# Two transformer blocks on one core: low halves between token tiles, identity transposes in the passages, other places for modulation fetches and for the experts' shares

## The chip, the core and the metric

The kernel runs on one core of a Trainium2 chip. The metric is the device time of one launch in microseconds; several launches of one build are made, and the median is given. Engines are named as in the profile: PE (TensorE), DVE (VectorE), ACT (ScalarE), POOL (GpSimd), SP (SyncE, which here only issues transfers).

## What is computed

The input is 256 tokens of width 1024 and one condition vector `c`. Two blocks follow each other, each of two layers.

```python
mods = einsum('bd,lde->lbe', silu(c), ada_w) + ada_b          # 6 vectors of 1024 per layer
for layer in range(2):                                        # first block
    sh1, sc1, g1, sh2, sc2, g2 = split(mods[layer], 6)
    h = rms_norm(x) * (1 + sc1) + sh1
    y = conv_fox_mixer(h) if layer == 0 else nsa_mixer(h)
    x = x + g1 * y
    h = rms_norm(x) * (1 + sc2) + sh2
    x = x + g2 * peer_ffn(h)          # 8 heads, 16 of 16384 experts each
for i in range(2):                                            # second block
    x = x + 0.5 * swiglu(rms_norm(x))                         # 1024 -> 2816 -> 1024
    x = x + concat(ssd(h), dilated_attention(h)) @ w_out      # h = rms_norm(x)
    x = x + 0.5 * swiglu(rms_norm(x))
```

In `peer_ffn` two key tables give 16 best scores each per head, their 256 sums give 16 picks, a softmax over the picks gives their shares, and each pick adds `share * gelu(x . u[e]) * v[e]`. The kernel computes it densely: all 16384 rows of `u` and `v` pass through PE, in tiles, and the shares are laid out as a sparse gate matrix.

## The kernel before

**Stages.** The program is a hand-scheduled list of instructions for each engine, with waits on semaphores. It goes through ten stages: mix0 (convolution and Fox attention), peer0, mix1 (the NSA mixer), peer1, ffnA0, ssd0, ffnB0, ffnA1, ssd1, ffnB1. The 256 tokens are two token tiles of 128. Activations stay in the chip's memory, and weights are streamed once.

**The ring.** All weights come as tiles of 128 x 1024 f32 (512 KB), named by their matrix and number: foxst (mix0's projections), foxo (its output), pq, pu, pv (the peer's queries, up and down), nsac, nsag, nsaq, nsak, nsaw, nsav, nsao (mix1) and so on. `sync_program` (L528) issues them on SP in one fixed order into the ring RING of NR = 5 buffers: tile n waits until tile n - 5 is used. The order is written out by the stages' lists, so everything on SP stands in one queue.

**Halves.** A product is made from a high half and a low half of both operands. ACT rounds each tile into HI (L506, NHL = 4 buffers), and DVE or POOL makes LOW = RING - HI (`lo_upto`, L519). The activations have the halves HTH and HTL. PE runs three products per tile: HTH with HI, HTL with HI, HTH with LOW (L772, L775, L780 in `project_two` for the first two tiles of a stage, L792 for the others, L810 and L843 for output tiles, L1960 and L1983 in the peer). Each is 8 matmuls of 128 x 256 or 4 of 128 x 512.

**Modulation.** The twelve vectors of the modulation are background work. `modulation_plan` ties items to tiles of the stream. A piece p has a "first" (POOL clears ACC at L551 and fetches the bias at L555), eight "slots" (DVE adds silu(c)_k times one 512 KB tile of ada_w to ACC, L571) and a "last" (PE sums over partitions at L600 or L606, and DVE finishes at L583 or L586). Pieces 2, 3, 4 lie in mix0 and piece 8 in mix1; their tiles don't go through the ring but into own buffers, nine in mix0 and four in mix1, fetched by SP at L535. `own_behind` says behind which ring tile, and an own fetch waits until the slot that had its buffer is done. The waits on SP, DVE and PE are in program order on each engine.

**Passage.** Between two stages the four quarters q = 2t + hf of the output y (token tile t, half hf) lie in four banks of the accumulation memory. `residual_vector` (DVE) first makes the LOW tiles up to the second tile of the next stage, then adds y to X: L890 in the second block, or L896 and L899 with a gate. ACT sums the squares (`norm_squares`, L656 for tile 0, L660 twice for tile 1), POOL takes the inverse roots (`norm_pool`, L671 to L681), DVE and ACT scale the rows (`norm_rows_vector` L688 for tile 0, L690 for tile 1, with ACT L663 for its last columns), and PE turns them in 8 transposes per token tile (`norm_tensor`, L706). ACT and DVE evict HTH (L722, L724, L743, L745), then HTL (L754, or L732 and L759 where there is a shift). PE has nothing else to do between the end of y and L706.

**The picks.** In the peer, `peer_experts` (DVE) finds, for token tile 0 and then for token tile 1, 16 top-16 lists over the keys, 8 over the sums and the experts' numbers, beside PE's up tiles j = 0 to 43. Behind tile SECOND_T = 44, ACT makes exp for both token tiles (L2104), and for each token tile in turn `peer_shares` makes the shares (L2197 to L2201), PE turns them (L2017), and DVE copies rows, columns and parts out (L2206 to L2214). Then the gates begin (L2233 to L2238 on DVE, L1946 on PE). exp and gelu are in different tables of ACT, and a change of table is an instruction of its own (ACT_TABLE_LOAD).

## Time and profile before

| | us |
|---|---|
| median of 3 runs | 3353.19 |
| lowest and highest | 3352.21, 3355.07 |
| the profiled execution | 3352.22 |
| its span, first to last instruction | 3350.4 |
| mean granted clock of PE, of full | 0.979 |
| busy: PE | 3200.2 (96%) |
| busy: DVE | 2408.6 (72%) |
| busy: ACT | 1662.8 (50%) |
| busy: POOL | 505.2 (15%) |

The profile is of one execution. The time of a run is some 2 us longer than the span. Busy times are sums over the span; matmuls overlap one another there and their ends are modelled, so a busy PE is not PE at its peak. The granted clock is given as a share of 2.4 GHz; 0.50 is 1.2 GHz. Line numbers are those of the kernel before.

### The profile page before, as it was taken

The page shows a single profiled execution, that of the slowest core. Times are in us where ns is not written, and L with a number is a line of the kernel's source. Part 1 is how long each engine was busy: PE and PEld are TensorE (multiplying, and loading weights), DVE is VectorE, ACT ScalarE, POOL GpSimd, SP SyncE. Part 2 cuts the span into 40 slices and gives each one's busy share as a digit, 9 for nine tenths or more (in the row PEclk, how much of TensorE's full clock was granted, in tenths as well). Part 3 has the DMA queues.
Part 4 walks back from the last instruction along what each step waited for, and adds up shares of the span by engine and source line. Part 5 has one row for each costly group of instructions (what it writes and reads, how often), then busy time and mean ns, then how long its engine had stood idle before and what let it go on. Part 6 is the DMA issues. An engine that isn't in the chain of part 4 may idle for free.

```text
span 3350.4 us, 56953 instructions
## 1 busy us (share of the span) xinstructions
PE 3200.2 (96%) x22530; PEld 2859.7 (85%) x22530; DVE 2408.6 (72%) x4140; ACT 1662.8 (50%) x2675; POOL 505.2 (15%) x363
## 2 busy tenths in 40 slices
PE   6899999999997889999999999999999999999999
PEld 6689877888887669987789998989869999898798
DVE  7879999776766569999966556558775555687754
ACT  3454555444454465455544544446554444465543
POOL 0269100000000258600000000001240000022300
PEclk8999999999998899999999999999999999999999
DMA  9445345677766215445566665555345655544355
GB/s 333 156 134 184 124 158 171 189 260 240 254 203 217 87 59 168 155 136 170 170 195 218 190 186 169 184 178 169 115 131 168 185 173 185 173 150 139 120 184 168
DMA packets 160534, 582.24 MB, mean 174 GB/s; under 512 B 18448, under 2 KB 20240, under 8 KB 160144
## 3 DMA queue, kind: packets, MB, share of 16 engines
q1 hardware_dynamic: 156528, 569.69, 53.3%
q10 hardware_dynamic: 3168, 8.35, 0.7%
q8 instruction: 181, 2.97, 0.3%
q0 software_dynamic: 576, 0.57, 0.1%
q14 instruction: 81, 0.66, 0.1%
HBM read 576.96 MB, written 1.05 MB: 173 GB/s over the span
## 4 chain that ended last, share of the span: by engine, by line
PE 86%; DVE 8%; ACT 2%; DMA 2%; issue 2%; POOL 1%; ACTq 0%; DVEq 0%; SPq 0%; POOLq 0%
PE P L1960 22%; PE P L792 21%; PE P L1983 21%; PE P L843 11%; PE P L1946 2%; DVE LOW L519 1%; DVE ssd_a L2768 1%; PE P L772 1%; PE P L706 1%; DVE mix_a L571 1%; ACT HI L506 1%; PE P L868 1%; PE P L775 1%; PE P L810 1%; PE P L1039 1%
## 5 line engine op out<-in xcount | busy, mean ns | idle before, releaser
L519 DVE TENSOR_TENSOR LOW<-RING,HI 128x1024 fp32r<-128x1024 f32 x882 | 1074.2, 1229 | 390.9 <-ACT HI L506 390.1
L506 ACT ACTIVATE HI<-RING 128x1024 fp32r<-128x1024 f32 x988 | 1037.2, 1053 | 388.9 <-DMA RING<-in_pu 157.5
L792 PE MATMUL P<-HTH,HI 128*128 128x256 f32 x2240 | 325.3, 288 | 18.8 <-ACT HI L506 13.9
L792 PE MATMUL P<-HTH,LOW 128*128 128x256 f32 x2240 | 317.2, 284 | 6.3 <-DVE LOW L519 6.1
L792 PEld LDWEIGHTS P<-HTH,HI 128*128 128x128 f32 x2240 | 291.9, 193 | 28.9 <-issue 18.7
L792 PE MATMUL P<-HTL,HI 128*128 128x256 f32 x2240 | 316.3, 284 | 0.0
L1960 PE MATMUL P<-HTH,HI 128*128 128x256 f32 x2048 | 299.8, 286 | 0.9 <-ACT HI L506 0.8
L792 PEld LDWEIGHTS P<-HTH,LOW 128*128 128x128 f32 x2240 | 290.3, 193 | 8.8 <-DVE LOW L519 8.8
L1960 PE MATMUL P<-HTL,HI 128*128 128x256 f32 x2048 | 291.0, 285 | 0.0
L792 PEld LDWEIGHTS P<-HTL,HI 128*128 128x128 f32 x2240 | 290.9, 193 | 0.0
L519 POOL TENSOR_TENSOR LOW<-RING,HI 128x1024 fp32r<-128x1024 f32 x106 | 279.0, 2653 | 62.4 <-ACT HI L506 62.4
L1960 PE MATMUL P<-HTH,LOW 128*128 128x256 f32 x2048 | 288.1, 284 | 0.0
L1960 PEld LDWEIGHTS P<-HTH,HI 128*128 128x128 f32 x2048 | 274.4, 191 | 14.4 <-issue 5.2
L1960 PEld LDWEIGHTS P<-HTL,HI 128*128 128x128 f32 x2048 | 265.2, 191 | 0.0
L1960 PEld LDWEIGHTS P<-HTH,LOW 128*128 128x128 f32 x2048 | 264.5, 191 | 0.0
L2052 ACT ACTIVATE peer_a<-P 128x256 f32<-128x256 f32 x256 | 97.7, 382 | 325.9 <-PE P L1960 325.8
L671 POOL TENSOR_SCALAR STAT<-STAT 128x1 f32<-128x1 f32 x10 | 2.2, 221 | 1100.0 <-DVE X L890 577.1
L2247 DVE TENSOR_TENSOR peer_a<-peer_a 128x256 f32<-128x256 f32 x256 | 159.4, 623 | 6.0 <-ACT peer_a L2052 5.9
L1983 PE MATMUL P<-LOW,peer_wh 128*128 128x512 f32 x512 | 150.2, 415 | 0.0
L551 POOL MEMSET ACC<- 128x1024 f32 x10 | 9.5, 954 | 923.7 <-PE P L1946 578.7
L2042 ACT ACTIVATE peer_a<-P 128x512 f32<-128x512 f32 x128 | 76.5, 597 | 134.2 <-PE P L1946 134.2
L1983 PE MATMUL P<-HI,peer_wh 128*128 128x512 f32 x512 | 138.2, 392 | 1.6 <-ACT peer_wh L2061 1.6
(434 smaller groups left out, 5101.5 us busy)
## 6 DMA issues: line engine op xcount, KB each, us to landing
RING<-in_pu SPq DMA_DIRECT2D x256, 512.0 KB, 3.9
RING<-in_pv SPq DMA_DIRECT2D x256, 512.0 KB, 3.6
RING<-in_ada SPq DMA_DIRECT2D x64, 512.0 KB, 4.8
...
```

The costliest lines, as they stand in the source:

```text
L506: act.activation(c.his[i % NHL], c.raw[m % NR], ACT.Copy).then_inc(*c.hi.at(("hi", m)))
L519: eng.tensor_tensor(c.low[m % NR], c.raw[m % NR], c.his[i % NHL].bitcast(F32), ALU.subtract).then_inc(*sig.at(("lo", m)))
L571: dve.scalar_tensor_tensor(out=acc, in0=c.own_tile(n) if own else c.raw[n % NR], scalar=c.silu_c[:, k:k + 1], in1=acc, op0=ALU.mult, op1=A ...
L706: m = pe.transpose(c.y[k // 2][:, k % 2 * 256 + t * 128:][:, 0:128], xn[:, t, k * 128:k * 128 + 128], c.const("ident"))
L792: m = pe.matmul(ps[:, 0:256], w[:, k * 128:k * 128 + 128], c.ht[h][:, k, :], start=i == 0 and k == 0, stop=i == 2 and k == 7)
L843: m = pe.matmul(c.y[q], lhs[1 if i == 1 else 0][:, t * 128:t * 128 + 128], (lo if i == 2 else hi)[:, hf * 512:hf * 512 + 512], start=i == ...
L1946: m = pe.matmul(f.gate_bank[:, 64 * t:64 * t + 64], f.is_row[g % 2][:, t // SIDE, :, t % SIDE], f.share[g % 2][q][:, t // SIDE, :, t % SID ...
L1960: m = pe.matmul(ps[:, 0:256], w[:, k * 128:k * 128 + 128], c.ht[h][:, k, :], start=i == 0 and k == 0, stop=i == 2 and k == 7)
L1983: m = pe.matmul(c.y[q], (f.wl(j) if i == 1 else f.wh(j))[:, t * 128:t * 128 + 128], (lo if i == 2 else hi)[:, hf * 512:hf * 512 + 512], st ...
L2042: act.activation(dst, c.psum(s, "gates", part, g).rearrange("p (t j) -> p t j", t=8), ACT.Copy, scale=1.0 / SHARE).then_inc(*c.act.at((s, ...
L2052: act.activation(f.act_of(c, j), c.psum(f.u, j)[:, 0:256], ACT.Gelu_apprx_tanh).then_inc(*c.act.at((f.s, "gelu", j), ("free", f.u, j)))
L2247: dve.tensor_tensor(ge, ge, f.gate_of(j), ALU.mult).then_inc(*c.dve.at((s, "weighed", j)))
```

## The change

It has four places.

1. In mix0 a modulation slot or another item is tied to every foxst tile but the first; before, foxst3 and foxst6 had none either. Later items come one or two tiles earlier, and the last sum (piece 4) two output tiles earlier. In mix1, piece 8 goes to nsac4 to nsac7 and nsaq0 to nsaq4 and nsaq6; before it had nsac2 to nsac7 and nsaq4 to nsaq7. `own_behind` places each own fetch at least five tiles behind the use that frees its buffer, and in mix1 the first ones behind nsac6.
2. `keep_clock` lets PE turn the identity matrix into a bank of its own: 28 times before it waits for the rows of token tile 0 in the passages into peer0, mix1, peer1 and ffnA0, 14 times in those into ssd0, ffnB0, ffnA1, ssd1 and ffnB1, and 3 times in all nine before the rows of token tile 1.
3. `residual_vector` makes the LOW tiles between token tile 0 and token tile 1.
4. In the peer, token tile 0's exp is made behind tile 28, its shares behind the 16 key lists of token tile 1, its transposes behind tile 34 and its parts behind the 8 lists of sums of token tile 1. Token tile 1 stays behind tile 44.

```diff
--- before.py
+++ after.py
@@ -16,7 +16,7 @@
 NR = 5
 NHL = 4
 AHEAD = {"act": 2, "dve": 1, "pool": 2}
-SECOND_T = 44
+EXP_T, FIRST_T, SECOND_T = 28, 34, 44
 SIDE = 2
 SHARE = 32768.0
 WHOLE = ("ada", "nsaw1")
@@ -336,14 +336,14 @@
             groups[10 * n + k].append(slots[k])
         groups[10 * n + 9].append(last)
     for t in FOX_ORDER:
-        if t[0] != "foxst" or t[1] > 8 or t[1] % 3:
+        if t != ("foxst", 0):
             after[t] = groups.pop(0) if groups else []
     assert not groups
     todo = of(6, 7, 9, 10, 5)
     spread(todo, [(("pv0", j), 1) for j in range(64, 127)])
     after["end", "peer0"] = todo
     todo = of(8)
-    spread(todo, [(("nsac", j), 1) for j in range(2, 8)] + [(("nsaq", j), 1) for j in (4, 5, 6, 7)])
+    spread(todo, [(("nsac", j), 1) for j in range(4, 8)] + [(("nsaq", j), 1) for j in (0, 1, 2, 3, 4, 6)])
     after["end", "mix1"] = todo
     todo = of(11)
     spread(todo, [(("pv1", j), 1) for j in range(64, 127, 3)])
@@ -411,12 +411,14 @@
             end = self.background.get(("end", s), [])
             self.stream += [(("ada", 8 * p + k), "") for what, p, k in end if what == "slot"]
         self.own_behind = {}
-        for order in (FOX_ORDER, [t for t, _ in stage_tiles("mix1")]):
+        for order, slots, begin in ((FOX_ORDER, OWN_SLOTS, 4), ([t for t, _ in stage_tiles("mix1")], OWN_LATE_SLOTS, 6)):
+            uses = []
             for place, t in enumerate(order):
                 for what, p, k in self.background.get(t, []):
                     if what == "slot":
-                        at = order[max(4, place - 3)]
-                        self.own_behind.setdefault(at, []).append(OWN.index(p) * 8 + k)
+                        free = uses[-slots] + 5 if len(uses) >= slots else begin
+                        self.own_behind.setdefault(order[max(free, place - 3)], []).append(OWN.index(p) * 8 + k)
+                        uses.append(place)
         self.place = {t: n for n, (t, _) in enumerate(self.stream)}
         assert len(self.place) == len(self.stream)
         halved = [n for n, (t, _) in enumerate(self.stream) if t[0] not in WHOLE]
@@ -691,14 +693,26 @@
         *c.dve.at((s, "rows", 1)))
 
 
+def keep_clock(pe, c, key, n):
+
+    ps = open_bank(pe, c, *key)
+    for k in range(n):
+        m = pe.transpose(ps[:, k % 4 * 128:k % 4 * 128 + 128], c.const("ident"), c.const("ident"))
+    m.then_inc(*c.pe.at(("free", *key)))
+
+
 def norm_tensor(pe, c, s):
 
     xn = norm_rows(c, s)
+    if s != STAGES[0]:
+        keep_clock(pe, c, ("clock", s, 0), 28 if s[:3] in ("pee", "mix") or s == "ffnA0" else 14)
     for q in range(4):
         if c.y_last[q] is not None:
             pe.wait_ge(*c.by("y_free", c.y_last[q], q))
         c.y_last[q] = s + "norm"
     for t in range(2):
+        if t and s != STAGES[0]:
+            keep_clock(pe, c, ("clock", s, 1), 3)
         pe.wait_ge(*c.by(s, "rows", t))
         for k in range(8):
             if t and k == ROWS_SPLIT // 128:
@@ -879,9 +893,9 @@
 def residual_vector(dve, c, s, name, scale, gate=None, gate_ready=None):
 
 
-    if s != STAGES[-1]:
-        lo_upto(dve, c, "dve", c.halved[c.turn[c.first_tile(STAGES[STAGES.index(s) + 1])] + 1])
     for t in range(2):
+        if t and s != STAGES[-1]:
+            lo_upto(dve, c, "dve", c.halved[c.turn[c.first_tile(STAGES[STAGES.index(s) + 1])] + 1])
         for hf in range(2):
             q = 2 * t + hf
             x = c.x[:, t, hf * 512:hf * 512 + 512]
@@ -2009,8 +2023,8 @@
             m.then_inc(*c.pe.at((s, "key_scores", t, hp)))
     for j in range(64):
         peer_up_tensor(pe, c, f, j, early_gates(j))
-        if j == SECOND_T:
-            for t in range(2):
+        for t in range(2):
+            if j == (FIRST_T, SECOND_T)[t]:
                 ps = open_bank(pe, c, s, "picks_turned", t)
                 pe.wait_ge(*c.by(s, "shares", t))
                 for q, src in enumerate((f.ei, f.ej, f.gg)):
@@ -2097,8 +2111,8 @@
         if j == 0:
             act.wait_ge(*c.by(s, "key_scores", 1, 3))
         peer_up_scalar(act, c, f, j)
-        if j == SECOND_T:
-            for t in range(2):
+        for t in range(2):
+            if j == (EXP_T, SECOND_T)[t]:
                 gg = f.gg[:, 128 * t:128 * t + 128]
                 act.wait_ge(*c.by(s, "shifted", t))
                 act.activation(gg, gg, ACT.Exp).then_inc(*c.act.at((s, "exp", t)))
@@ -2147,6 +2161,8 @@
         if h % 4 == 0:
             dve.wait_ge(*c.by(s, "scores", t, h // 4))
         top16(dve, c, sc[:, h, :], sv[:, h, :], si[:, h, :])
+    if t:
+        peer_shares(dve, c, f, 0)
     sf = f.sf[:, 256 * t:256 * t + 256]
     dve.wait_ge(*c.dve.last())
     dve.tensor_copy(sf.rearrange("p (q a h) -> p h q a", q=2, a=16), si.rearrange("p (h q) a -> p h q a", q=2))
@@ -2160,6 +2176,8 @@
     dve.wait_ge(*c.dve.last())
     for h in range(8):
         top16(dve, c, cd[:, h * 256:h * 256 + 256], cv[:, h, :], ci[:, h, :])
+    if t:
+        peer_parts(dve, c, f, 0)
     cit, cut = f.ci[:, 128 * t:128 * t + 128], f.cu[:, 128 * t:128 * t + 128]
     ca, cb = f.ca[:, 128 * t:128 * t + 128], f.cb[:, 128 * t:128 * t + 128]
     dve.wait_ge(*c.dve.last())
@@ -2200,6 +2218,10 @@
     dve.wait_ge(*c.dve.last())
     dve.tensor_tensor(gg, gg, st.unsqueeze(2).broadcast_to([128, 8, 16]), ALU.mult).then_inc(
         *c.dve.at((s, "shares", t)))
+
+
+def peer_parts(dve, c, f, t):
+    s = f.s
     dve.wait_ge(*c.by(s, "picks_turned", t))
     ps = c.psum(s, "picks_turned", t)
     for q, dst in enumerate((f.row, f.col)):
@@ -2262,8 +2284,8 @@
     peer_experts(dve, c, f, 0)
     peer_experts(dve, c, f, 1)
     feed(dve, c, "dve", f.u, SECOND_T)
-    peer_shares(dve, c, f, 0)
     peer_shares(dve, c, f, 1)
+    peer_parts(dve, c, f, 1)
     dve.wait_ge(*c.by(s, "parts", 1))
     for j in range(SECOND_T + 1, 64):
         for g in early_gates(j):
```

**SP, the start of mix1.** The order of the transfers before (nsac, nsag, nsaq are ring tiles, mix_a<-in_ada the own tiles of piece 8):

```order
L528 DMA RING<-in_nsac 128x1024 x5
L535 DMA mix_a<-in_ada 128x1024 x5
L528 DMA RING<-in_nsac 128x1024 x3
L528 DMA RING<-in_nsag 128x1024
L528 DMA RING<-in_nsaq 128x1024 x2
L535 DMA mix_a<-in_ada 128x1024
L528 DMA RING<-in_nsaq 128x1024
L535 DMA mix_a<-in_ada 128x1024
L528 DMA RING<-in_nsaq 128x1024
L535 DMA mix_a<-in_ada 128x1024
L528 DMA RING<-in_nsaq 128x1024 x4
```

and now:

```order
L530 DMA RING<-in_nsac 128x1024 x7
L537 DMA mix_a<-in_ada 128x1024 x4
L530 DMA RING<-in_nsac 128x1024
L530 DMA RING<-in_nsag 128x1024
L530 DMA RING<-in_nsaq 128x1024 x2
L537 DMA mix_a<-in_ada 128x1024
L530 DMA RING<-in_nsaq 128x1024
L537 DMA mix_a<-in_ada 128x1024
L530 DMA RING<-in_nsaq 128x1024
L537 DMA mix_a<-in_ada 128x1024
L530 DMA RING<-in_nsaq 128x1024 x2
L537 DMA mix_a<-in_ada 128x1024
```

Seven nsac tiles instead of five are issued ahead of the own tiles, four own tiles instead of five follow at once, and the later own tiles come one at a time between nsaq tiles.

**PE, the passage into ffnA1.** Before (L810 ends y, L706 turns the rows, L772 begins the next stage):

```order
L810 MATMUL P<-HI,ffnB_h 128x512
L810 MATMUL P<-HI,ffnB_l 128x512
L810 MATMUL P<-LOW,ffnB_h 128x512
L706 MATMUL P<-CST,ffnA_a 128x128 x16
L772 MATMUL P<-HTH,HI 128x256 x8
L775 MATMUL P<-HTH,LOW 128x256 x8
```

and now:

```order
L824 MATMUL P<-HI,ffnB_h 128x512
L824 MATMUL P<-HI,ffnB_l 128x512
L824 MATMUL P<-LOW,ffnB_h 128x512
L700 MATMUL P<-CST 128x128 x14
L720 MATMUL P<-CST,ffnA_a 128x128 x8
L700 MATMUL P<-CST 128x128 x3
L720 MATMUL P<-CST,ffnA_a 128x128 x8
L786 MATMUL P<-HTH,HI 128x256 x8
L789 MATMUL P<-HTH,LOW 128x256 x8
```

The 16 transposes have become 8 and 8, with 14 identity transposes ahead of the first 8 and 3 ahead of the second.

**DVE, the same passage.** Before (L519 makes LOW, L890 adds a quarter of y, L688 and L690 are the rows):

```order
L2370 TENSOR_TENSOR ffnB_l<-ffnB_a,ffnB_h 128x256
L519 TENSOR_TENSOR LOW<-RING,HI 128x1024 x23
L890 SCALAR_TENSOR_TENSOR X<-P,X 128x512 x4
L688 TENSOR_SCALAR ffnA_a<-X,STAT 128x1024
L690 TENSOR_SCALAR ffnA_a<-X,STAT 128x640
L743 TENSOR_SCALAR HTH<-P,CST 128x256 x4
```

and now:

```order
L2392 TENSOR_TENSOR ffnB_l<-ffnB_a,ffnB_h 128x256
L521 TENSOR_TENSOR LOW<-RING,HI 128x1024 x22
L904 SCALAR_TENSOR_TENSOR X<-P,X 128x512 x2
L521 TENSOR_TENSOR LOW<-RING,HI 128x1024
L904 SCALAR_TENSOR_TENSOR X<-P,X 128x512 x2
L690 TENSOR_SCALAR ffnA_a<-X,STAT 128x1024
L692 TENSOR_SCALAR ffnA_a<-X,STAT 128x640
L757 TENSOR_SCALAR HTH<-P,CST 128x256 x4
```

The last LOW stands between the two quarters of token tile 0 and those of token tile 1.

**DVE, picks of peer0.** Before, from the end of the experts (L2188) and LOW of the tile behind on:

```order
L2188 TENSOR_TENSOR peer_a<-peer_a 128x128
L519 TENSOR_TENSOR LOW<-RING,HI 128x1024
L2197 TENSOR_REDUCE STAT<-peer_a 128x8
L2199 RECIPROCAL STAT<-STAT 128x8
L2201 TENSOR_TENSOR peer_a<-peer_a,STAT 128x128
L2206 CAST peer_ij<-P 128x128 x2
L2209 TENSOR_SCALAR peer_g<-P 128x128
L2211 SCALAR_TENSOR_TENSOR peer_eq<-P,peer_g 128x128
L2214 CAST peer_g<-peer_eq 128x128
L2197 TENSOR_REDUCE STAT<-peer_a 128x8
L2199 RECIPROCAL STAT<-STAT 128x8
L2201 TENSOR_TENSOR peer_a<-peer_a,STAT 128x128
```

and now, first behind the key lists of token tile 1 (L2148, L2150 are parts of such a list, L2168 begins the sums):

```order
L2148 MAX peer_a<-peer_a 128x8
L2150 MAX_INDEX peer_a<-peer_a 128x8
L2215 TENSOR_REDUCE STAT<-peer_a 128x8
L2217 RECIPROCAL STAT<-STAT 128x8
L2219 TENSOR_TENSOR peer_a<-peer_a,STAT 128x128
L2168 CAST peer_a<-peer_a 128x8x32
L2171 TENSOR_TENSOR peer_a<-peer_a 128x2048
L2142 MAX peer_a<-peer_a 128x8
```

and from the end of the experts on:

```order
L2206 TENSOR_TENSOR peer_a<-peer_a 128x128
L521 TENSOR_TENSOR LOW<-RING,HI 128x1024
L2215 TENSOR_REDUCE STAT<-peer_a 128x8
L2217 RECIPROCAL STAT<-STAT 128x8
L2219 TENSOR_TENSOR peer_a<-peer_a,STAT 128x128
L2228 CAST peer_ij<-P 128x128 x2
L2231 TENSOR_SCALAR peer_g<-P 128x128
L2233 SCALAR_TENSOR_TENSOR peer_eq<-P,peer_g 128x128
L2236 CAST peer_g<-peer_eq 128x128
L2255 TENSOR_TENSOR peer_eq<-peer_iota,peer_ij 128x512
```

Behind the experts there is one leg of shares and parts instead of two, and the first gate (L2255) follows it.

## Rows read from the trace of the kernel before

**Rows 1.** The page's chain that ended last, by engine and line.

```profile
PE 86%; DVE 8%; ACT 2%; DMA 2%; issue 2%; POOL 1%; ACTq 0%; DVEq 0%; SPq 0%; POOLq 0%
PE P L1960 22%; PE P L792 21%; PE P L1983 21%; PE P L843 11%; PE P L1946 2%; DVE LOW L519 1%; DVE ssd_a L2768 1%; PE P L772 1%; PE P L706 1%; DVE mix_a L571 1%; ACT HI L506 1%; PE P L868 1%; PE P L775 1%; PE P L810 1%; PE P L1039 1%
```

**Rows 2.** The table of waits, PE: total, times, longest in us.

```profile
PE P L792 <- ACT HI L506: 13.9, 1, 13.9
```

**Rows 3.** Timeline of mix1's start: start, length, engine and line, [idle before <-releaser].

```profile
1023.99 18.29 SPq L535 DMA_DIRECT2D mix_a<-in_ada  x5
...
1036.31 1.19 POOL L1852 TENSOR_TENSOR mix_a<-mix_a 128x480 f32<-128x480 f32 x1 [19.95 <-DMA mix_a<-in_cmpb]
...
1040.65 1.28 DVE L571 SCALAR_TENSOR_TENSOR ACC<-mix_a,MOD,ACC 128x1024 f32<-128x1024 f32 x1 [8.51 <-issue]
1042.33 1.38 SPq L528 DMA_DIRECT2D RING<-in_nsac  x3
...
1047.99 2.05 PE L792 MATMUL P<-HTH,HI 128*128 128x256 f32 x8 [13.91 <-ACT HI L506]
...
1059.94 1.12 PE L792 MATMUL P<-HTL,HI 128*128 128x256 f32 x8
...
1060.90 1.12 PE L792 MATMUL P<-HTH,LOW 128*128 128x256 f32 x8
```

**Rows 4.** Windows of mix1: busy of PE, PEld, DVE, ACT, POOL; clock, DMA share, GB/s.

```profile
1022.00:1037.00 15.00, 12.08 (x101) 11.88 (x99) 9.64 (x20) 4.47 (x7) 0.69 (x1) 0.97 1.00 394
```

**Rows 5.** Windows of the passage into mix1, same columns.

```profile
1016.00:1019.00 3.00, 3.00 (x16) 2.97 (x15) 1.28 (x3) 1.70 (x4) 0.36 (x1) 0.50 0.00 0
```

**Rows 6.** Timeline, PE's transposes (L706) in the passages into mix1, ffnB0, ffnA1.

```profile
1015.52 3.56 PE L706 MATMUL P<-CST,mix_a 128*128 128x128 f32 x16 [4.65 <-DVE mix_a L688]
...
2511.48 3.65 PE L706 MATMUL P<-CST,ffnB_a 128*128 128x128 f32 x16 [2.86 <-DVE ffnB_a L688]
...
2707.02 1.07 PE L706 MATMUL P<-CST,ffnA_a 128*128 128x128 f32 x8 [2.76 <-DVE ffnA_a L688]
```

**Rows 7.** Timeline of the passage into ffnA1, DVE and ACT.

```profile
2701.36 1.22 DVE L519 TENSOR_TENSOR LOW<-RING,HI 128x1024 fp32r<-128x1024 f32 x1 [1.57 <-ACT HI L506]
...
2702.50 2.49 DVE L890 SCALAR_TENSOR_TENSOR X<-P,X 128x512 f32<-128x512 f32 x4
...
2703.81 1.06 ACT L656 ACTIVATE HTL<-X 128x1024 fp32r<-128x1024 f32 x1 [2.49 <-DVE X L890]
...
2707.70 0.55 DVE L690 TENSOR_SCALAR ffnA_a<-X,STAT 128x640 f32<-128x640 f32 x1 [0.82 <-POOL STAT L681]
```

**Rows 8.** Timeline of the passage into peer0.

```profile
177.40 1.84 PE L606 MATMUL P<-CST,ACC 128*128 128x1 f32 x16
179.28 0.17 DVE L586 SCALAR_TENSOR_TENSOR MOD<-P,CST 128x8 f32<-128x8 f32 x1 [5.49 <-PE P L606]
...
185.72 3.65 PE L706 MATMUL P<-CST,peer_a 128*128 128x128 f32 x16 [6.48 <-DVE peer_a L688]
```

**Rows 9.** Window of mix0's first products, columns as above.

```profile
53.00:80.00 27.00, 26.12 (x214) 25.51 (x213) 24.82 (x34) 9.86 (x15) 0.00 (x0) 1.00 0.93 336
```

**Rows 10.** Timeline of mix0, DVE.

```profile
128.34 1.28 DVE L571 SCALAR_TENSOR_TENSOR ACC<-mix_a,MOD,ACC 128x1024 f32<-128x1024 f32 x1 [2.68 <-issue]
```

**Rows 11.** Timeline behind tile 44 of peer0, PE and DVE.

```profile
353.26 0.73 PE L2017 MATMUL P<-CST,peer_a 128*128 128x128 f32 x3 [3.08 <-DVE peer_a L2201]
...
355.22 0.28 DVE L2197 TENSOR_REDUCE STAT<-peer_a 128x8 f32<-128x128 f32 x1
...
356.20 0.87 PE L2017 MATMUL P<-CST,peer_a 128*128 128x128 f32 x3 [2.21 <-DVE peer_a L2201]
...
358.42 0.43 DVE L2233 TENSOR_TENSOR peer_eq<-peer_iota,peer_ij 128x512 f16<-128x512 f16 x1
...
360.27 1.01 PE L1946 MATMUL P<-peer_pc,ACC 128*128 128x64 f16 x16 [2.34 <-DVE peer_pc L2238]
```

**Rows 12.** Timeline of peer0, ACT at tile 28.

```profile
304.15 0.38 ACT L2052 ACTIVATE peer_a<-P 128x256 f32<-128x256 f32 x1 [1.55 <-PE P L1960]
```

## The prediction

> **What bounds the kernel now.** I read the page's chain first: 86% of what ended last lies on TensorE (PE) [rows 1]. So an edit can pay in two ways only: it shortens a wait of PE, or a stretch in which PE runs on its lower clock. The table of waits says where to look: a single wait of 13.9 us for a high half [rows 2]. The timeline shows what stands behind it [rows 3], and the windows show the clock: 1.00 is 2.4 GHz, 0.50 is 1.2 GHz [rows 4, 5]. Everything below is summed against the profiled execution, 3352.22 us (span 3350.4); the median of the three runs is 1.0 us above it.
>
> **Part 1, the fetches in mix1: 12.5 us.** SP issues five nsac tiles and then five own ada tiles. The fifth has to wait until slot (8, 0) has freed its buffer, so that group stands on SP for 18.29 us, and nsac5 is fetched only at 1042.33. PE therefore starts nsac5 at 1047.99 after 13.91 us of waiting, and at the lower clock: 2.05 us for 8 matmuls, where a group at the higher clock takes 0.96 (from 1059.94 to 1060.90) [rows 3]. Slot (8, 0) itself was late, since it needs the bias, which POOL fetches only after L1852, and L1852 waited for in_cmpb until 1036.31 while the DMA engines were at a share of 1.00 [rows 3, 4].
> The change moves seven nsac tiles ahead of four own tiles and nothing on SP waits there. nsac5 and nsac6 are issued at about 1024 to 1025; behind them come four own tiles and nsac7. From 1024 on some 9 tiles of 512 KB and the rest of in_toep are moved at the 394 GB/s of that window [rows 4], 1.33 us a tile, so nsac7 lands by about 1040 and its three products could start at about 1041. DVE is the next limit. Slot (8, 0) stands in front of LOW of nsac7, and its bias comes about where it came (DVE L571 at 1040.65; I take up to 3 us later, because the memory set and bias moved behind nsac4 and nsac5 share the queues). So LOW of nsac7 is there by about 1045.1, and PE waits 1.6 to 3.3 us at nsac7, depending on how long the lower clock holds its first products back. Its LOW group and nsag's three follow, 4 x 0.96, at a clock not yet quite back: through at 1049.3. Before, nsag was through at 1061.9 [rows 3]. **Gain 12.5**, with ends 4 (the wait only moves, rival C) and 13.5 (slot (8, 0) comes on time). The moved slots stand in the q part, where DVE does 1.22 + 0.95 + 1.28 = 3.4 us a tile (LOW, the bias products, the slot) against about 3.6 of PE: cost 0, and were that cover gone, 0.2 for each of six tiles.
>
> **Part 2, the transposes: 10 us.** In each of the nine passages PE stops while DVE adds the residual and forms the first rows: 6.48 us (peer0), 4.65 (mix1), 2.86 (ffnB0), 2.76 (ffnA1) [rows 6, 8]; peer1 and ffnA0 are like mix1, the ssd passages like ffnB0. Behind that wait the granted clock is 0.50, for the 16 transposes and the first matmuls [rows 5]. At the lower clock 16 transposes take 3.65 us, 0.228 each; at the higher one 8 take 1.07, 0.134 each [rows 6]. 28 of the new ones are 3.8 us, 14 are 1.9, 3 are 0.4: at the higher clock all fit into the waits they stand in. So they cost nothing, if they count as work for the clock. That a row decides: in mix1 the clock came back at about 1019.0, just as the 16 transposes of L706, and nothing else, had run for 3.56 us [rows 5, 6]; in peer0 L706 runs 3.65 at 0.50 and is followed by the same return.
> What it gives: in ffnB0 the second rows are there at 2512.7 and their 8 transposes end at 2513.8 instead of 2515.1. Now the evictions bound it. HTH starts 0.9 to 1.0 earlier (ACT and DVE, 1.7 us each), the first four groups of matmuls end 2.0 earlier, HTL 1.0 earlier. Between 1.0 and 2.0 I take 1.5, for ffnA0, ffnB0 and ffnB1. ssd0 and ssd1 had the high clock for a part and get 1.15 each, ffnA1, whose first 8 transposes ran fast [rows 6], 1.05. In peer0, mix1 and peer1 the eight shifted columns on ACT (0.6 each) and their low parts follow one another; they start 0.7 earlier, and that is the gain: 3 x 0.7. **Sum 3 x 1.5 + 2 x 1.15 + 1.05 + 3 x 0.7 = 10**, ends 0 (rival B) and 14 (2.0 in the ffn kind).
> The Trainium skill ("TensorE: Matmul & The Clock Gate", section "Part 4: PE-mode transpose") speaks against this part: it says that the full clock does not engage for transposes, since they do not count as PE being busy in the same way. By that rule this term would be 0 and the sum 10 smaller; the rows of mix1 don't bear it out, but they can't exclude it, as matmuls followed at once.
>
> **Part 3, LOW between the token tiles: 3.2 us.** In ffnA1 DVE made LOW of the second next tile (1.22) up to 2702.5 and only then the four L890; ACT's squares of token tile 0 waited for the second of these until 2703.81 [rows 7]. y of tile 0 was complete over a microsecond earlier. Now tile 0 is added 1.2 earlier and LOW lies in front of tile 1, whose end stays at 2705.0. The squares start 1.2 earlier, the first rows 1.05 earlier. The two L660 of tile 1 then start on their data, 0.45 earlier than 2704.87 and 2705.48, and the second rows (2707.70) come about 0.6 earlier. Of that passage kind there are five: **5 x 0.6 = 3.0**; ends 0 and 5. In mix1 and ffnA0, where four pairs of 1.33 us bound DVE itself, it is 0.1 each. In peer0 and peer1 the LOW of the next stage is POOL's, nothing moves.
>
> **Part 4, modulation in mix0: 1.6 us.** The last sum (L606, 1.84 us on PE) stood at the end of mix0 and DVE waited for it with the whole residual, until 179.28 [rows 8]. It now runs two output tiles earlier. It stays on PE's path (y is 1.7 to 1.8 later there), but the residual starts with y: L606 takes over from the last matmul of L810 at 177.40 [rows 8], and y of the first quarter is there about 1 us before that. So it starts up to 2.7 earlier. DVE beside POOL's LOW is slower there, so I take **2.1**, ends 0 and 2.7. Against it: the two slots added behind foxst3 and foxst6 cost 1.28 each on DVE in a stretch where DVE is busy for 24.82 of 27 us and PE for 26.12 [rows 9]: at most 2.6, and half of it, 1.2, is taken; the waits for bias and slots at 124 to 138 (2.68 in front of L571 at 128.34 [rows 10]) come earlier and give 0.75 back. Net 1.6. The seven own tiles in one go behind foxst4, 9.3 us of traffic instead of 6.7, are ahead of a ring with five tiles in it: cost 0, or up to 2.6 if the ring runs dry.
>
> **Part 5, the picks: 3.4 us.** Behind tile 44 of peer0 PE waits 3.08 (L2017), 2.21 (L2017 again) and 2.34 (L1946) [rows 11]. Tile 1's leg runs from 355.22 to the first pick at 358.42, 3.2 us. With tile 0 done during tile 1's picks, only tile 1's leg is left behind tile 44, but DVE's experts end later: it waits about 1.1 for exp of tile 0, since ACT has gelu of tile 28 at 304.15 and then a table load and the exp, about 1.6, and it does the shares (355.22 until just before 356.20, 0.85) and the parts (1.3, up to 358.42) there [rows 11, 12]. So the experts end at about 352.3 instead of 349.0, LOW and tile 1's leg follow, and the picks start at 356.7: **gain 1.7** of the 3.2, ends 0 and 3.2. PE and DVE are both full for the 75 us behind, so a gain there carries. Two peers: 3.4. The two more table loads of each peer lie on ACT, which works for half of each tile: cost 0, and up to 2.6 a peer if ACT were the limit.
>
> **Sum**: 12.5 + 10 + 3.2 + 1.6 + 3.4 = 30.7 us, which gives 3352.2 - 30.7 = 3321.5, and with the 1.0 of the median **3322 us**.
>
> **Rivals.**
> A (my forecast, chance 0.67): as summed, within 3316 to 3328.
> B, the clock falls all the same (0.15): the transposes fit but the clock is 0.50 behind them. For it: the clock's return in mix1 may belong to the matmuls that followed at once. Against it: it came just as the transposes ended [rows 5, 6]. Part 2 then gives 0, and the overrun is small: 28 at 0.228 are 6.4 us against 4.65 of wait. Time: 3322 + 10 = 3332, and up to 3334 with the overrun.
> C, the wait in mix1 moves (0.12): slot (8, 0) is held up by the bias and LOW of nsac7 behind it, PE falls to the lower clock again, part 1 gives 4 instead of 12.5. For it: POOL's 19.95 us of waiting, which nothing in the change shortens [rows 3]. Against: two more tiles of work (5.8 us) are now ahead of it. Time 3322 + 8.5 = 3330.5.
> D, more than summed (0.04): ends above reached in parts 2 and 3: 3314.
> E, slower (0.02): SP's queue. It is one queue in fixed order, and the row of 18.29 us shows what an own fetch that waits for its buffer does to the ring behind it. In mix0, 15 of the 24 own fetches wait for a slot's release. If each of them held the ring for more than 30.7 / 15 = 2.0 us on PE's path, the gain is gone; at 2.5 us each the time is 3352 + 7 = 3359. Against it: with slots nine uses back and the fetch five places behind, the release is over long before; the page shows no such wait in mix0 now. That the change doesn't do what it says is excluded by the order of instructions, apart from B.
>
> **Numbers.** 3322 is the likeliest case's time. The range takes in B, C and a part of D: **3314 to 3334**; outside lie both B and C together (3340) and E. The measurement can tell 0.2%, 6.7 us, from no change. Faster by more than that: A to D, and B with C, 0.96; within 0.2% 0.02; slower 0.02.
>
> **What would show it.** Part 1: no wait of PE in front of nsac5, 1 to 4 us at nsac7, nsag through at about 1049 counted from mix1's start. Part 2: clock near 1.00 in the passages, L706 at 0.134 each, L700 at 0.134 too; were B right, L700 at 0.228 and clock 0.50. Part 3: the squares 1.2 and the second rows 0.6 earlier against the last y. Part 4: no wait of DVE for L606's sum in the passage. Part 5: one leg behind tile 44, picks 1.7 earlier against the end of tile 44. I am wrong if the time is above 3334 or below 3314, and wrong in the reasons if part 1 gives under 8 or part 2 under 5.

## The result, and the profile after

The changed kernel took 3335.3 us (median of 4, 3329.1 to 3336.9) beside 3353.5 (4 runs) for the kernel before: ratio 0.9949, 95% interval 0.9936 to 0.9962. On a second chip it was 3339.0 (5 runs) beside 3350.4 (10 runs), ratio 0.9965, 0.9951 to 0.9978. So 11 to 18 us were gained where the prediction had 31, and 3335.3 lies 1.3 us above the upper end of its range, 3339.0 lies 5.0 above it. The direction was right, the size was not.

The profiled execution took 3336.90 us (span 3335.1, mean granted clock 0.989 where it had been 0.979). Its page, the chain that ended last by engine and line (line numbers are now the changed kernel's, 2 to 22 higher):

```profile
PE 83%; DVE 10%; DMA 2%; ACT 2%; issue 2%; POOL 1%; ACTq 0%; DVEq 0%; POOLq 0%
PE P L806 22%; PE P L1997 20%; PE P L1974 19%; PE P L857 11%; PE P L1960 2%; DVE LOW L521 1%; DVE ssd_a L2790 1%; PE P L786 1%; DMA RING<-in_pv 1%; DMA RING<-in_pu 1%; PE P L824 1%; PE P L882 1%; ACT HI L508 1%; PE P L1053 1%; PE P L789 1%
```

PE's share fell from 86 to 83% [rows 1]; transfers for pu and pv have come in. In the table of waits the one wait of 13.9 us of [rows 2] has become three, 4.2 us together, the longest 2.9, and a line is there that was in no trace before, L1974 behind L2233:

```profile
PE P L2031 <- DVE peer_a L2219: 6.1, 2, 3.1
...
PE P L806 <- ACT HI L508: 4.2, 3, 2.9
...
PE P L1974 <- DVE peer_eq L2233: 3.6, 2, 1.8
```

**mix1.** The timeline (start, length, engine and line, [idle before <-releaser]):

```profile
1014.96 3.22 PE L700 MATMUL P<-CST 128*128 128x128 f32 x28
...
1029.53 1.93 SPq L537 DMA_DIRECT2D mix_a<-in_ada  x4
...
1033.28 0.33 SPq L530 DMA_DIRECT2D RING<-in_nsac  x1
...
1047.22 1.06 ACT L508 ACTIVATE HI<-RING 128x1024 fp32r<-128x1024 f32 x1 [6.06 <-DMA RING<-in_nsac]
...
1048.42 1.19 PE L806 MATMUL P<-HTH,HI 128*128 128x256 f32 x8 [2.88 <-ACT HI L508]
1048.57 1.28 DVE L573 SCALAR_TENSOR_TENSOR ACC<-mix_a,MOD,ACC 128x1024 f32<-128x1024 f32 x1 [4.87 <-issue]
```

These answer to [rows 3]. The own fetches are four and take 1.93 us on SP instead of 18.29. PE waits 0.56 us at nsac5 and 2.88 at nsac7, and not 13.91. ACT had to wait for the transfer of nsac7, which was issued at 1033.28 and landed at 1047.20. The identity transposes (L700) run at 0.115 us each (28 in 3.22), faster than the 0.134 I had taken.

**The passage into ffnA1**, against [rows 6, 7]: the turned rows take 1.07 and 1.09 and no transpose is at the lower clock.

```profile
2691.52 1.69 PE L700 MATMUL P<-CST 128*128 128x128 f32 x14
...
2693.35 1.07 PE L720 MATMUL P<-CST,ffnA_a 128*128 128x128 f32 x8
...
2695.01 1.09 PE L720 MATMUL P<-CST,ffnA_a 128*128 128x128 f32 x8 [0.27 <-DVE ffnA_a L692]
```

**The passage into peer0**, against [rows 8]. The residual starts at 178.8, as the prediction wanted, but two of its four L913 take 1.23 and 2.16 us instead of 0.69, while POOL makes two LOW tiles. The first rows stand at 187.09; before they stood at 185.72.

```profile
177.35 5.61 POOL L521 TENSOR_TENSOR LOW<-RING,HI 128x1024 fp32r<-128x1024 f32 x2 [5.50 <-ACT HI L508]
...
179.48 1.23 DVE L913 TENSOR_TENSOR X<-X,mix_a 128x512 f32<-128x512 f32 x1
...
181.35 2.16 DVE L913 TENSOR_TENSOR X<-X,mix_a 128x512 f32<-128x512 f32 x1
...
187.09 1.06 PE L720 MATMUL P<-CST,peer_a 128*128 128x128 f32 x8 [2.35 <-DVE peer_a L690]
```

**The picks of peer0**, against [rows 11, 12]:

```profile
307.12 0.29 DVE L2215 TENSOR_REDUCE STAT<-peer_a 128x8 f32<-128x128 f32 x1 [1.13 <-ACT peer_a L2118]
...
322.17 0.49 PE L2031 MATMUL P<-CST,peer_a 128*128 128x128 f32 x3
...
332.76 0.29 DVE L2233 SCALAR_TENSOR_TENSOR peer_eq<-P,peer_g 128x128 f32<-128x128 f32 x1
333.09 2.12 DVE L2236 CAST peer_g<-peer_eq 128x128 f16<-128x128 f32 x1
...
333.11 1.21 PE L1974 MATMUL P<-HTH,HI 128*128 128x256 f32 x8 [1.82 <-DVE peer_eq L2233]
...
356.59 0.61 PE L2031 MATMUL P<-CST,peer_a 128*128 128x128 f32 x3 [3.07 <-DVE peer_a L2219]
...
358.54 0.43 DVE L2255 TENSOR_TENSOR peer_eq<-peer_iota,peer_ij 128x512 f16<-128x512 f16 x1
```

Behind tile 44 one leg is gone, as forecast. But the first pick starts at 358.54 (before 358.42), in a trace that is 0.9 behind already at the start of the stage (rounding 36, below). DVE waits 1.13 for exp, as forecast; and PE, which turned tile 0's picks at 322.17, stands still for 1.82 us at 333.11 until DVE's L2233 has read them. The cast behind it takes 2.12 us, where tile 1's takes 0.23.

**Where the time went.** ACT rounds 988 tiles (L508, L506 before) in the same order in every kernel, so the starts of the same rounding can be set against one another in two traces. The table gives, for seven stretches between such starts, how much longer (+) or shorter than in the first profile of before they were, in us; the first row is counted from the start of the span. The last column is of kernels in which nothing of that stretch was touched (runs below).

| stretch (numbers of the roundings) | forecast | the change | again | untouched |
|---|---|---|---|---|
| mix0, passage into peer0 (0 to 36) | -2.3 | +0.9 | +2.4 | -0.2 to +2.3 |
| peer0 up to the down part, picks (36 to 180) | -1.7 | -1.1 | +1.0 | +0.1 to +0.6 |
| peer0, down part (180 to 292) | 0 | +4.4 | +2.2 | -1.3 to +5.1 |
| passage into mix1 and its start (292 to 317) | -13.3 | -10.2 | -8.9 | -0.3 to +0.6 |
| rest of mix1, passage into peer1 (317 to 336) | -0.7 | -1.6 | -0.5 | -3.4 to -0.9 |
| peer1 (336 to 588) | -1.7 | +0.1 | +1.3 | 0.0 to +0.8 |
| the second block (588 to 987) | -11.0 | -8.0 | -8.7 | -5.3 to 0.0 |

### The profile page after: what moved, and what is told of

Same layout as the page of the kernel before. It is cut to its first block, busy times and chain, and to the rows that moved or that the text cites. A ratio compares the mean times of both kernels' runs of the same rounds, so it can differ in the third digit from the quotient of the medians.

```text
span 3335.1 us, 57375 instructions
## 1 busy us (share of the span) xinstructions
PE 3218.4 (97%) x22739; PEld 2871.8 (86%) x22739; DVE 2410.0 (72%) x4140; ACT 1665.9 (50%) x2679; POOL 503.8 (15%) x363
## 4 chain that ended last, share of the span: by engine, by line
PE 83%; DVE 10%; DMA 2%; ACT 2%; issue 2%; POOL 1%; ACTq 0%; DVEq 0%; POOLq 0%
PE P L806 22%; PE P L1997 20%; PE P L1974 19%; PE P L857 11%; PE P L1960 2%; DVE LOW L521 1%; DVE ssd_a L2790 1%; PE P L786 1%; DMA RING<-in_pv 1%; DMA RING<-in_pu 1%; PE P L824 1%; PE P L882 1%; ACT HI L508 1%; PE P L1053 1%; PE P L789 1%
## 5 line engine op out<-in xcount | busy, mean ns | idle before, releaser
L508 ACT ACTIVATE HI<-RING 128x1024 fp32r<-128x1024 f32 x988 | 1035.6, 1053 | 374.7 <-DMA RING<-in_pu 153.3
L1974 PE MATMUL P<-HTH,HI 128*128 128x256 f32 x2048 | 300.4, 287 | 6.0 <-DVE peer_eq L2233 3.6
L806 PEld LDWEIGHTS P<-HTH,LOW 128*128 128x128 f32 x2240 | 291.1, 193 | 10.6 <-DVE LOW L521 10.6
L1974 PEld LDWEIGHTS P<-HTH,HI 128*128 128x128 f32 x2048 | 274.9, 191 | 20.0 <-issue 6.7
L1974 PE MATMUL P<-HTL,HI 128*128 128x256 f32 x2048 | 290.9, 285 | 0.0
L1974 PE MATMUL P<-HTH,LOW 128*128 128x256 f32 x2048 | 288.3, 284 | 0.0
L1974 PEld LDWEIGHTS P<-HTL,HI 128*128 128x128 f32 x2048 | 265.2, 191 | 0.0
L1974 PEld LDWEIGHTS P<-HTH,LOW 128*128 128x128 f32 x2048 | 264.5, 191 | 0.0
```

The lines of the kernel that those rows point to most:

```text
L508: act.activation(c.his[i % NHL], c.raw[m % NR], ACT.Copy).then_inc(*c.hi.at(("hi", m)))
L806: m = pe.matmul(ps[:, 0:256], w[:, k * 128:k * 128 + 128], c.ht[h][:, k, :], start=i == 0 and k == 0, stop=i == 2 and k == 7)
L1974: m = pe.matmul(ps[:, 0:256], w[:, k * 128:k * 128 + 128], c.ht[h][:, k, :], start=i == 0 and k == 0, stop=i == 2 and k == 7)
```

## The experiments

Each kernel was timed beside the kernel before on the same chip. The parts are those of the prediction. Single runs of every kernel, the one before too, scatter over up to 15 us, so differences of 2 to 3 us between medians tell little and smaller effects are read from one stretch of the traces.

**again**: the changed kernel once more.

> The changed kernel once more. Its profiled execution lost 4.3 us against before between the first down tile of peer0 and the passage into mix1, where the change alters no instruction; its four runs spread over 8 us. Theory 'traffic': that loss is chance of the transfers, so this profile shows another number there, the time lies anywhere in 3328 to 3337, and runs spread over several us again. Rival 'shift': the loss belongs to the kernel, it is 4 us there again (3 to 5).

3338.97 us (3335.8 to 3341.8), ratio 0.9965. The down part of peer0 was 2.2 longer than in the first profile of before, not 4.4. See before_again.

**before_again**: the kernel before once more.

> The kernel before once more, for a second profile. Between the first down tile of peer0 and the passage into mix1 (325 us, no instruction of it touched) eight profiles of other kernels took from 1.3 less to 5.1 more than the first profile of before. If that is chance of the transfers, this one lies in the same scatter, not at 0, and the time's scatter is as wide as the others' (8 us and more).

3351.34 us (3346.3 to 3357.9, 11 runs), ratio 0.9997 (0.9988 to 1.0006). The down part took 4.1 more than in the first profile with not one instruction changed. So the 4.4 us lost there by the change lie inside the scatter of a kernel that has no change in it; what varies there was not found. The two differences of medians, 18 and 11, hold such scatter too. The whole trace is 5.5 us longer at its last rounding.

**only_mix1**: the kernel before with part 1 alone.

```diff
-    spread(todo, [(("nsac", j), 1) for j in range(2, 8)] + [(("nsaq", j), 1) for j in (4, 5, 6, 7)])
+    spread(todo, [(("nsac", j), 1) for j in range(4, 8)] + [(("nsaq", j), 1) for j in (0, 1, 2, 3, 4, 6)])
```
(with the change's `own_behind` for mix1)

> The kernel before with only mix1's modulation plan and own fetches of the change. From the trace of the changed kernel: no fetch waits on SP, one wait of PE of 2 to 3 us at nsac7, gain of 10 to 12 us between the passage into mix1 and the one into peer1, nothing elsewhere. The part of peer0 behind the first down tile is as in the kernel before (0 within 1) if the 2 to 4 us lost there in all profiles of the change come from the change; if they are chance of the transfers it is 2 to 4 slower here too.

3339.59 us (11 runs), ratio 0.9972 (0.9963 to 0.9981), beside 3351.17: the medians differ by 11.6, the ratio says 9.4. In its trace the start of mix1 is 10.6 shorter, with waits of PE of 2.20 at nsac5 and 0.59 at nsac7, and the down part of peer0 0.7 longer, inside the scatter. Part 1 is most of what the change gives.

**own_later**: from pq_low_dve (below), the first own fetches of mix1 behind nsag.

```diff
-        ... [t for t, _ in stage_tiles("mix1")], OWN_LATE_SLOTS, 6)):
+        ... [t for t, _ in stage_tiles("mix1")], OWN_LATE_SLOTS, 8)):
```

> pq_low_dve with mix1's first four own fetches issued behind nsag instead of behind nsac6, so nsac7 and nsag are not behind 2 MB of them. Theory 'transfers' (nsac7 landed 15 us after its issue, and that is PE's last wait in mix1): nsac7's high half comes some 4 us earlier, PE's waits in front of nsac7 and its LOW go from 1.8 us to under 1, gain 0.5 to 2. Rival 'slot in front of LOW': slot (8, 0) stands ahead of LOW of nsac7 on DVE and its own tile now lands later, PE waits for that LOW instead, 0 to 4 us slower.

3334.76 us, ratio 0.9947 (0.9934 to 0.9960); the kernel it comes from had 0.9939, so no gain. The timeline shows both halves of the answer: ACT has nsac7 and nsag rounded by 1042.2, with no wait of PE left for the high half of nsac7, and then PE waits 3.90 us for LOW, since slot (8, 0), L573, comes first on DVE, at 1047.43.

```profile
1041.14 1.06 ACT L508 ACTIVATE HI<-RING 128x1024 fp32r<-128x1024 f32 x1 [0.21 <-DMA RING<-in_nsag]
...
1041.50 0.61 POOL L557 DMA_DIRECT2D ACC<-in_adab  x1 [0.29 <-POOL ACC L553]
...
1047.43 1.28 DVE L573 SCALAR_TENSOR_TENSOR ACC<-mix_a,MOD,ACC 128x1024 f32<-128x1024 f32 x1 [5.18 <-issue]
...
1049.90 1.94 PE L806 MATMUL P<-HTH,LOW 128*128 128x256 f32 x8 [3.90 <-DVE LOW L521]
```

The rival was right in the wait, not in what holds the slot: its own tile had landed at 1042.40, but its bias, fetched by POOL at 1041.50, landed only at 1047.35. In the changed kernel too the slot (1048.57) begins as its bias has landed (1048.49). So two things end at about the same time in front of nsac7, its transfer and the bias of the slot ahead of its LOW, and bringing the first forward alone gave nothing; the bias was not moved in any run. The stretch from 292 to 317 was 1.8 longer than in pq_low_dve.

**no_clock**: the change without the identity transposes.

```diff
-    if s != STAGES[0]:
-        keep_clock(pe, c, ("clock", s, 0), 28 if s[:3] in ("pee", "mix") or s == "ffnA0" else 14)
...
-        if t and s != STAGES[0]:
-            keep_clock(pe, c, ("clock", s, 1), 3)
```

> The changed kernel without the identity transposes. If they hold the clock: 0.50 stretches again behind the passages and 7 to 10 us slower than the changed kernel. If they do nothing for the clock (the rule that transposes don't count): same time within 2 us.

3339.36 us, ratio 0.9966 (0.9952 to 0.9979), beside 0.9965 with them: nothing by the medians. The trace says why. In ffnA0 the clock fell and 16 transposes took 3.65; in ffnA1, with LOW between the token tiles, PE waits only 1.67 and both groups run at the higher clock without any help (L716 is the turning of rows here):

```profile
2052.55 3.65 PE L716 MATMUL P<-CST,ffnA_a 128*128 128x128 f32 x16 [4.53 <-DVE ffnA_a L690]
...
2693.94 1.07 PE L716 MATMUL P<-CST,ffnA_a 128*128 128x128 f32 x8 [1.67 <-DVE ffnA_a L690]
2695.61 1.09 PE L716 MATMUL P<-CST,ffnA_a 128*128 128x128 f32 x8 [0.60 <-DVE ffnA_a L692]
```

The time is the one that was expected if the transposes did nothing, but the reason is another: the transposes do hold the clock (only_clock), and where the earlier LOW had already shortened the wait there was little left to lose. Of the five passages behind ffnA0 only ffnB0 still lost the clock, for its second rows (1.66).

**only_low**: the kernel before with LOW between the token tiles alone.

```diff
-    if s != STAGES[-1]:
-        lo_upto(dve, c, "dve", ...)
     for t in range(2):
+        if t and s != STAGES[-1]:
+            lo_upto(dve, c, "dve", ...)
```

> The kernel before with only LOW moved between the token tiles. Theory 'covered twice': PE's idle time before the first rows falls from 2.8 to 1.7 in the second block's five plain passages, the clock stays at 1.00 in most of them, and the five give 4 to 7 us together, more than the 3.0 of the prediction; mix1, ffnA0 and the peers give 0. Rival: rows come 0.6 earlier and the clock falls as before, 3.0.

3347.54 us (12 runs), ratio 0.9993 (0.9985 to 1.0002). The second block is 5.9 shorter than in the first profile of before. By the time, a gain isn't clear of noise. The wait in front of the first rows of ffnA1 is 1.66 instead of 2.76 [rows 6], and both groups of transposes run fast:

```profile
2703.85 1.07 PE L706 MATMUL P<-CST,ffnA_a 128*128 128x128 f32 x8 [1.66 <-DVE ffnA_a L688]
...
2705.52 1.09 PE L706 MATMUL P<-CST,ffnA_a 128*128 128x128 f32 x8 [0.60 <-DVE ffnA_a L690]
```

**only_clock**: the kernel before with the transposes alone.

> The kernel before with only the identity transposes. Theory 'covered twice': the transposes hold the clock in all nine passages, but without them the earlier LOW already keeps it in four of the five passages of the second block, so alone they give 1.0 to 1.5 us in each of ffnA0, ssd0, ffnB0, ffnA1, ffnB1 and about 0 in ssd1, 5 to 7 us in those six. Rival 'no gain': the evictions bound the passages and the six give under 2.

3348.12 us (12 runs), ratio 0.9987 (0.9978 to 0.9997). All transposes of rows from mix1 to ffnB1 take 1.06 to 1.09 a group; in peer0 the first group still took 1.94. In ffnA0, whose 16 row transposes took 3.65 in no_clock:

```profile
2062.55 3.22 PE L698 MATMUL P<-CST 128*128 128x128 f32 x28
...
2067.54 1.07 PE L718 MATMUL P<-CST,ffnA_a 128*128 128x128 f32 x8 [1.77 <-DVE ffnA_a L688]
...
2069.03 1.09 PE L718 MATMUL P<-CST,ffnA_a 128*128 128x128 f32 x8
```

The second block is 7.5 shorter. But in three kernels in which neither the transposes nor LOW were touched it was also shorter than in the first profile of before: 1.5 (only_mix0), 3.1 (only_mix1), 5.3 us (only_picks). A part of the reason stands in ffnB0, where only_mix1 has the instructions of before. It turned its first rows at the higher clock after the same wait of 2.84 us, where [rows 6] has 16 at the lower after 2.86 (L708 is L706 of before):

```profile
2499.45 1.06 PE L708 MATMUL P<-CST,ffnB_a 128*128 128x128 f32 x8 [2.84 <-DVE ffnB_a L690]
2500.74 1.97 PE L708 MATMUL P<-CST,ffnB_a 128*128 128x128 f32 x8 [0.23 <-DVE ffnB_a L692]
```

**clock_longer**: from pq_low_dve, 44 instead of 28 transposes.

> pq_low_dve with 44 identity transposes instead of 28 in the passages into peer0, mix1, peer1 and ffnA0. The 28 end 1.5 to 2.4 us before the rows come, and in peer0 the clock still fell in half of the profiles. 44 take 5.1 us at 0.115: theory 'the rest of the wait still costs': clock at 1.00 in all four passages, first rows delayed by at most 0.4, 0 to 1 us faster. Rival: the overrun delays the rows' transposes by more than it gives, up to 1.6 us slower.

3331.96 us (6 runs), ratio 0.9939 (0.9926 to 0.9952), the same as with 28. With 28 the first group had still been turned at the lower clock in peer1 by the change (1.94) and in peer0 by again (1.94), and in peer0 of pq_low_dve the second took 1.85. With 44 the clock is at 1.00 in all four passages when the rows are turned, peer0 among them:

```profile
182.07 4.96 PE L700 MATMUL P<-CST 128*128 128x128 f32 x44
186.87 1.04 PE L720 MATMUL P<-CST,peer_a 128*128 128x128 f32 x8
```

The first rows are turned without a wait now, 4.80 us behind the start of the identity transposes where pq_low_dve has 4.90, and nothing is gained that a median can tell.

**mix0_as_before**: the change with `if t[0] != "foxst" or t[1] > 8 or t[1] % 3` and mix0's own fetches as before.

> The changed kernel with mix0's modulation plan and own fetches as before. My account of the two traces: the two added slots cost 2.6 us in foxst's part, the earlier last sum gives back about 2 in the passage. So this is the same within 1.5 us as the changed kernel; if the prediction's term (1.6 gained) holds, it is 1.6 slower; if only the cost is real, 2 faster.

3339.11 us (6 runs), ratio 0.9967 (0.9954 to 0.9979), beside 0.9965 for again: the same. All adds of the passage take 0.69 again, since the wait for the last sum holds them until POOL has finished. Up to rounding 36 it was 2.1 behind the first profile of before, the changed kernel 2.4 in the same batch.

**only_mix0**: the kernel before with mix0's plan alone.

> The kernel before with only mix0's plan and fetches of the change. Expected from the trace of the changed kernel: foxst's part 1.4 us longer, the residual of the passage starts with y but two of its L899 run beside POOL's LOW and take 2 to 2.7 us together more than 1.4, so the first rows of peer0 stand 1 to 2 us later than before in all: slower by 1 to 2. By the prediction: 1.6 faster.

3351.66 us (11 runs), ratio 0.9999 (0.9990 to 1.0008): nothing. In its trace two of the four adds take 1.25 and 2.14 us.

**pq_low_dve**: from turn_later (below), LOW of the first two pq tiles on DVE, ahead of the residual.

```diff
-        order = [((f"pq{l}", j), "pool") for j in range(8)] + ...
+        order = [((f"pq{l}", j), "dve" if j < 2 else "pool") for j in range(8)] + ...
...
-        if t and s != STAGES[-1]:
+        if s != STAGES[-1] and t == (STAGES[STAGES.index(s) + 1][:4] != "peer"):
```

> turn_later with the LOW of the first two pq tiles of each peer made by DVE ahead of the residual instead of by POOL. Theory 'POOL's LOW slows DVE's add': all eight L913 of the two passages take 0.69 instead of 1.2 to 2.75, and the first rows come 0.5 to 1.2 earlier though DVE has 2.4 us more work there; 1 to 2 us faster than turn_later in all. Rival: the adds are slow for another reason, they stay at 1.2 to 2.75 and the passages are up to 2.4 us longer each.

3330.08 us (3328.8 to 3334.2), ratio 0.9939 (0.9926 to 0.9953), the lowest median of all. All eight adds take 0.69, although DVE has two more LOW to make. The first rows of peer0 are turned at 185.83, in turn_later at 187.69; 1.1 of these 1.9 us lie ahead of the end of y, 0.7 behind it:

```profile
176.09 3.49 DVE L521 TENSOR_TENSOR LOW<-RING,HI 128x1024 fp32r<-128x1024 f32 x3
...
180.22 0.69 DVE L913 TENSOR_TENSOR X<-X,mix_a 128x512 f32<-128x512 f32 x1
...
181.54 0.69 DVE L913 TENSOR_TENSOR X<-X,mix_a 128x512 f32<-128x512 f32 x1
...
185.83 1.07 PE L720 MATMUL P<-CST,peer_a 128*128 128x128 f32 x8 [1.68 <-DVE peer_a L690]
```

Against turn_later the two passages, from the end of y to the end of the 48th matmul of the stage behind, are 1.4 and 0.7 shorter; the first holds a difference of the clock too. The ratio of turn_later, 0.9942, is too near to this one to tell them apart.

**only_picks**: the kernel before with part 5 alone.

> The kernel before with only the first tile's shares moved. From the trace of the changed kernel: PE waits 1.8 us for the bank held by tile 0's turned picks, DVE 1.1 for exp, and one of two legs behind tile 44 goes: 0.5 to 1.0 gained in each peer, 1 to 2 in all, where the prediction had 3.4.

3349.22 us (12 runs), ratio 1.0000 (0.9990 to 1.0009). In the stretches with the picks it is 2.2 longer (peer0) and 1.4 shorter (peer1), where untouched kernels are 0 to 0.8 longer. The part gives nothing that can be told.

**turn_early**: the change with FIRST_T = 31.

> The changed kernel with tile 0's transposes behind tile 31 instead of 34. Theory 'held bank': the bank is held 3 tiles (8.6 us) longer, PE waits for DVE's parts(0) from tile 34 or 35 on for up to 10 us instead of 1.8 in each peer, PE falls to the lower clock, and since DVE's experts set the end of that stretch about half of it is hidden: 5 to 9 us a peer, 10 to 18 slower in all. Rival 'the wait is no bank': same time.

3356.23 us (11 runs), ratio 1.0012 (1.0003 to 1.0021), 17 us above the median of again. The wait of 3.6 us has become 20.9, in both peers:

```profile
PE P L1974 <- DVE peer_eq L2233: 20.9, 2, 10.5
```

The bank it is: 8.6 us more of holding it cost 8.7 us more of wait in each peer, and the stretches with the picks are 8.0 and 8.8 us longer than in again, so nearly all of it was lost, the upper end of what was expected.

**turn_later**: the change with `EXP_T, FIRST_T, SECOND_T = 27, 37, 44`.

> The changed kernel with tile 0's exp behind tile 27 instead of 28 and its transposes behind tile 37 instead of 34. Theory 'held bank': PE waits 1.8 us (and 2.1 us of delay) for the bank that holds tile 0's turned picks until DVE's parts(0), and DVE waits 1.1 for exp; both waits go, about 2 to 3 us of gain in each peer, 4 to 5 in all. Rival 'DVE bound': the picks start where DVE is ready, so only the 1.1 us per peer of waiting for exp is gained, 2.2 in all.

3333.17 us (3324.9 to 3334.7), ratio 0.9942 (0.9929 to 0.9956) beside 0.9965 for again: 7.7 us by the ratios, 5.8 by the medians; the two intervals overlap only from 0.9951 to 0.9956. Beside the first pair of the changed kernel (0.9949) it is 2.3 by the ratios. In the trace neither wait is left, and the stretches with the picks are 2.6 (peer0) and 2.7 us (peer1) shorter than in again. The parts of tile 0 now start at 333.61, and their last cast still takes 1.97:

```profile
333.61 0.47 DVE L2228 CAST peer_ij<-P 128x128 f16<-128x128 f32 x2
...
334.64 1.97 DVE L2236 CAST peer_g<-peer_eq 128x128 f16<-128x128 f32 x1
```

## Why the prediction was wrong, part by part

**Part 1, the fetches (12.5).** Right in mechanism and nearly in size: 10.2, 8.9 and 10.6 in three traces, with at most 0.8 of part 2 in it. The step that was 2 us off is "nsac7 lands by about 1040". In the trace of the change, moved back by the 4.3 us that it is late at rounding 292, nsac7 lands at 1042.9 and its first products start at 1044.2, not 1041. The queue was already later at nsac5, which took 10.1 us from issue to landing, so the transfers ahead of it were counted too low. PE's waits for nsac5 and nsac7 are 3.4 us together (again 4.7, only_mix1 2.8), where I had none and 1.6 to 3.3. Slot (8, 0) began 3.7 us later than before, where I had taken up to 3, and would hold LOW back if nsac7 came sooner (own_later).

**Part 2, the transposes (10).** This is the first large miss. The step that failed is the price of a passage, 10 us in all, where the runs show some 2.5 on top of part 3. First, I took each passage's loss of clock from the one trace and called it what the passage costs. The clock at the same place differs from trace to trace with the same instructions: in ffnB0 16 transposes at the lower clock, or 8 fast ones and 8 slow (only_mix1).

Second, parts 2 and 3 were added although they cure the same wait: only_clock has 7.5 less in the second block, only_low 5.9, both together 8.0 and 8.7, where I had 11.0, and no_clock shows that with LOW moved the clock mostly stays up by itself in the plain passages. Against the untouched kernels (0.0 to 5.3 less) both together are worth some 3 to 9 us.

The passages alone tell it closer. Counted from the end of y to the end of the 48th matmul of the stage behind, the second block's six are together 7.6 to 8.1 us shorter than in the first profile of before in each of the eight traces with both parts, 5.9 in only_low, 6.0 in no_clock and 6.0 in only_clock; in the four traces without either (before_again, only_mix0, only_mix1, only_picks) they are between 0.1 longer and 3.1 shorter, by the draw of the clock and of the wait. So both parts are worth 5 to 8 us there, and the transposes on top of LOW 2.0, with 0.5 in mix1. Taken so, on top of part 3, part 2 gave under 5, and by the prediction's own sign it was wrong in its reasons.

I had also priced ssd1 like ssd0 without its rows; there before's transposes ran at the higher clock already, and it gained nothing. Rival B fell all the same: the transposes do hold the clock, at 0.115 us each, in every passage from mix1 on in only_clock. All row transposes from mix1 on ran in 1.06 to 1.09 us a group of 8 there, against 16 in 3.65 without [rows 6]. The Trainium skill's rule ("TensorE: Matmul & The Clock Gate", section "Part 4: PE-mode transpose"), that the full clock does not engage for transposes, doesn't hold here. By it the identity transposes would have changed nothing.

**Part 3, LOW (3.2).** In ffnA1 of only_low the first rows came 1.1 us earlier against the end of y, as worked out, the second 0.7 (0.6 worked out), and the passage gave 1.4 to 1.6 us in ssd0, ffnB0, ffnA1 and ffnB1 of only_low, more than the 0.6, since the shorter wait also kept the clock. This is the part of part 2 that had been counted there.

**Part 4, mix0 (1.6).** Nothing: 0 by the time of only_mix0 and of mix0_as_before. Up to rounding 36 only_mix0 is 1.1 behind, inside the -0.2 to 2.3 of kernels without the part, so a loss isn't shown either. The step that failed is "the residual starts with y ... I take 2.1". It did start with y, but beside POOL's LOW, and its two adds lost 0.54 + 1.47 us, in again 2.06 in one. I had seen such adds and kept 0.6 for them. The row in [rows 8] was free of it only because waiting for L606 had let POOL finish. The added slots cost about what was taken: by rounding 17 the kernels with them are 1.2 to 1.9 behind (without them -0.2 to 0.2), against the 1.2 taken.

**Part 5, the picks (3.4).** The second large miss: 0. The step that failed is a resource left out. The bank into which PE turns tile 0's picks is not free until DVE has read them, and DVE reads them only behind 8 more lists. PE comes to that bank again behind three more tiles and waits 1.8 us in each peer. turn_early (20.9 us of wait) and turn_later (none) settle it. With both waits gone (turn_later) each peer is 1.4 to 1.7 shorter than in the first profile of before, near the 1.7 predicted. A smaller term was left out too: the parts of tile 0 run beside POOL's LOW, and their last cast took 2.12 us instead of 0.23. DVE's experts end at 354.34, 5.2 us later than before (4.3 counted from rounding 36) and not 3.3.

**The sum** by traces: part 1 about 10, parts 2 and 3 about 6, parts 4 and 5 about 0, some 16 in all, which lies between the two measured differences (11 and 18). What stays open is why the clock and the wait of a passage differ from one execution to the next, and with it the size of parts 2 and 3 to better than 2 us. The range failed since it took in one rival at a time, and all of parts 1, 2, 4 and 5 were short together.
